# A hybrid decoder step on one core: five matmuls a k tile, and block products that add up in PSUM

## The reference

```
h = modulate(rms_norm(x));  x = x + 0.5 * gate1 * swiglu(h, gate, up, down)      # ffn1, hidden width 2816
h = modulate(rms_norm(x));  z = h @ w_in
x = x + gate2 * (merge(conv branch, linear attention branch) @ w_out)            # "out"
h = modulate(rms_norm(x));  x = x + 0.5 * gate3 * swiglu(h, gate, up, down)      # ffn2
y = modulate(rms_norm(x));  swiglu(h) = (silu(h @ w_gate) * (h @ w_up)) @ w_down
```

## Time and profile before

| | us |
|---|---|
| median of three runs | 1432.65 |
| the runs | 1431.9 to 1434.09 |
| span of the profiled execution (the page gives no other time for it) | 1432.1 |
| TensorE busy | 1389.1 (97%) |
| DVE busy | 977.2 (68%) |
| ACT busy | 539.3 (38%) |

### The profile page before, as it was taken

How to read it: one execution, slowest core, us unless ns; L and a number is a source line. 1 busy time by engine, 2 the same in 40 slices (tenths; PEclk the granted TensorE clock), 3 DMA queues, 4 the chain that set the end, 5 groups by cost and what they waited for, 6 DMA issues and landing times.

```text
span 1432.1 us, 28796 instructions
## 1 busy us (share of the span) xinstructions
PE 1389.1 (97%) x11782; PEld 1344.0 (94%) x11782; DVE 977.2 (68%) x1731; ACT 539.3 (38%) x797; POOL 80.2 (6%) x120
## 2 busy tenths in 40 slices
PE   6999999999999999999999999999999999999996
PEld 5899999999998999999899897999899999999996
DVE  6446675357547588998998997854554776456745
ACT  5423343224336222524243237422352344224433
POOL 6100000010001000000000000100000000000000
PEclk9999999999999999999999999999999999999998
DMA  9754646454364223213334453626312332323321
GB/s 322 237 177 155 205 149 206 147 168 142 103 208 142 89 88 93 89 60 104 125 128 146 136 169 127 220 91 198 104 59 74 92 117 89 114 76 106 101 77 60
DMA packets 132701, 189.49 MB, mean 132 GB/s; under 512 B 4621, under 2 KB 112545, under 8 KB 132386
## 3 DMA queue, kind: packets, MB, share of 16 engines
q1 hardware_dynamic: 111388, 112.54, 25.0%
q0 software_dynamic: 17136, 66.87, 14.0%
q10 hardware_dynamic: 4070, 8.57, 1.6%
HBM read 173.73 MB, written 15.18 MB: 132 GB/s over the span
## 4 chain that ended last, share of the span: by engine, by line
PE 84%; DVE 10%; ACT 3%; issue 2%; DMA 1%; POOL 0%; DVEq 0%; ACTq 0%
PE pu L646 51%; PE pu L828 13%; PE pu L817 11%; PE pu L660 2%; PE pg L690 2%; DVE w_lo L1680 1%; DMA work<-in_w_ada 1%; PE pg L1064 1%; ACT w_hi L1227 1%; DVE d L2106 1%; DVE w_lo L1969 1%; DVE work L2216 1%; PE pg L726 0%; DVE work L2215 0%; DVE work L2227 0%
## 5 line engine op out<-in xcount | busy, mean ns | idle before, releaser
L1680 DVE TENSOR_TENSOR w_lo<-raw,w_hi 128x1024 fp32r<-128x1024 f32 x152 | 186.1, 1225 | 255.5 <-ACT w_hi L1227 255.4
L1227 ACT CAST w_hi<-raw 128x1024 fp32r<-128x1024 f32 x152 | 158.9, 1046 | 412.0 <-PE pu L646 373.0
L646 PE MATMUL pu<-h_hi,w_hi 128*128 128x260 f32 x1408 | 288.4, 286 | 4.6 <-DVE work L2381 2.8
L646 PE MATMUL pu<-h_hi,w_lo 128*128 128x260 f32 x1408 | 284.1, 283 | 0.0
L646 PE MATMUL pu<-h_lo,w_hi 128*128 128x260 f32 x1408 | 283.3, 283 | 0.0
L646 PEld LDWEIGHTS pu<-h_hi,w_hi 128*128 128x128 f32 x1408 | 217.7, 189 | 8.7 <-DVE w_lo L1680 4.8
L646 PEld LDWEIGHTS pu<-h_hi,w_lo 128*128 128x128 f32 x1408 | 217.4, 189 | 0.0
L646 PEld LDWEIGHTS pu<-h_lo,w_hi 128*128 128x128 f32 x1408 | 217.2, 189 | 0.0
L2106 DVE SCALAR_TENSOR_TENSOR d<-u,cw,d 128x512 f32<-128x512 f32 x240 | 163.2, 745 | 0.1
L646 PE MATMUL pu<-f_hi,w_hi 128*128 128x260 f32 x704 | 142.9, 284 | 0.0
L646 PE MATMUL pu<-f_hi,w_lo 128*128 128x260 f32 x704 | 141.8, 283 | 0.0
(11 more groups left out here) (352 smaller groups left out, 2369.7 us busy)
## 6 DMA issues: line engine op xcount, KB each, us to landing
raw_a<-in_w_ada POOLq DMA_DIRECT2D x30, 1024.0 KB, 7.9
raw<-in_w_in SPq DMA_DIRECT2D x28, 1024.0 KB, 5.2
raw<-in_ffn_up SPq DMA_DIRECT2D x22, 1024.0 KB, 5.3
raw<-in_ffn_gate SPq DMA_DIRECT2D x21, 1024.0 KB, 5.3
raw<-in_ffn_down SPq DMA_DIRECT2D x16, 1024.0 KB, 5.1
gates_d<-sg ACTq DMA_DIRECT2D x24, 260.0 KB, 2.4
raw<-in_ffn_down SPq DMA_DIRECT2D x8, 768.0 KB, 4.4
work<-gates_d POOLq DMA_DIRECT2D x2, 2080.0 KB, 8.8
```

What stands on the lines that cost most here:

```text
L646: last = mm(pu[p][:, e, 0:HALF], w[p][:, k, :], m[:, k, e * HALF:(e + 1) * HALF], start=(k == 0 and j == 0), stop=(k == k_tiles - 1 and j ...
L1227: nc.scalar.copy(w_hi[p][:], raw[:, slot, :, p * P:(p + 1) * P]).then_inc(s_hi, 1)
L1680: V.tensor_tensor(w_lo[p][:], raw[:, slot, :, p * P:(p + 1) * P], w_hi[p][:].bitcast(F32), ALU.subtract).then_inc(s_lo, 1)
```

## The change

1. The down units and "out" are computed by `unit_uneven`: LEFT = 276 columns lie in one bank, the other REST = 244 twice in the other bank. w_hi meets h_hi's and h_lo's 244 columns in one matmul of 2 x 244 = 488 columns, whose two sums lie side by side; w_lo h_hi is added to the first of them. That makes five matmuls a k tile: 276, 488, 276, 276, 244. So that one operand can take in both, h_hi and h_lo become halves of one tensor, and f_hi and f_lo too.
2. `residual` adds both sums of 244: three scalar_tensor_tensors (236, 276 and 236 columns) and three small steps, with waits on a new semaphore between.
3. P1, P6, P7 and P4 are accumulated in one bank, and P5 and P3 in another. ACT copies the running sum out as p1, u2 and u3 and takes P4's by its Silu directly; DVE keeps three additions (c11 = p1 + P2, c22 = u3 + P5, c12 = u2 + (P5 + P3)). P2 lies in the other pair's first bank, and the pairs change roles from turn to turn. U0A comes before P4 and P3. ACT's Silu of the second tile is in two halves.
4. At the first turn of a group the wait for `s_evac[1]` stands ahead of P2.

Two semaphores of the spilled rows of x are made one, without another order. In the diff the up blocks' code (`up_half`, the halves of `up_unit`), DVE's three additions (in point 3) and renamed waits are left out.

```diff
+LEFT = 276
+REST = N - LEFT
...
-P1, P2, P6, P5, P7, P4, P3, U0A, U0B, U1A, U1B = range(TURN)
+P1, P2, P6, P5, P7, U0A, P4, P3, U0B, U1A, U1B = range(TURN)
+UP_BLOCKS = (U0A, U0B, U1A, U1B)
...
-        h_hi = sb("h_hi", [P, KT, N], F32R)
-        h_lo = sb("h_lo", [P, KT, N], F32R)
+        h2 = sb("h2", [P, 2, KT, N], F32R)
+        h_hi, h_lo = h2[:, 0], h2[:, 1]
...
+        f2, work = overlay(("f2", [P, 2, KT, N], F32R), ("work", [P, BF], F32))
...
+            def unit_uneven(n, p, both, k_tiles=KT, ready=None):
+
+                weights_and_psum(n, p)
+                hi, lo = both[:, 0], both[:, 1]
+                left, rest = pu[p][:, 0, 0:LEFT], pu[p][:, 1, 0:2 * REST]
+                for k in range(k_tiles):
+                    if ready is not None:
+                        s, v, first = ready
+                        if k == 0 and first > 1:
+                            pe.wait_ge(s, v + first)
+                        elif k >= first or k == 0:
+                            pe.wait_ge(s, v + k + 1)
+                    start, stop = k == 0, k == k_tiles - 1
+                    mm(left, w_hi[p][:, k, :], hi[:, k, 0:LEFT], start=start, stop=False)
+                    mm(rest.rearrange("p (s n) -> p s n", s=2), w_hi[p][:, k, :], both[:, :, k, LEFT:N],
+                       start=start, stop=False)
+                    mm(left, w_hi[p][:, k, :], lo[:, k, 0:LEFT], start=False, stop=False)
+                    mm(left, w_lo[p][:, k, :], hi[:, k, 0:LEFT], start=False, stop=stop)
+                    last = mm(rest[:, 0:REST], w_lo[p][:, k, :], hi[:, k, LEFT:N], start=False, stop=stop)
+                last.then_inc(s_done, 1)
...
-            def product(j, bank, hi, lo):
+            def product(j, bank, hi, lo, start=True):
 
                 pe.wait_ge(s_blo, j + 1)
                 for k in range(4):
                     for n, (w, m) in enumerate(((w_hi, hi), (w_hi, lo), (w_lo, hi))):
                         last = mm(bank, w_block(w, j)[:, k, :], m[:, k, :],
-                                  start=(k == 0 and n == 0), stop=(k == 3 and n == 2))
+                                  start=(start and k == 0 and n == 0), stop=(k == 3 and n == 2),
+                                  skip_group_check=not start)
                 last.then_inc(s_bd, 1)
...
-                    a0, a1, b0, b1 = (pu[p][:, e, 0:HALF] for p in range(2) for e in range(2))
+                    own, other = it % 2, 1 - it % 2
+                    a, b, c = pu[own][:, 0, 0:HALF], pu[other][:, 0, 0:HALF], pu[own][:, 1, 0:HALF]
                     m = ADA_UP[g] + 2 * it if which == 1 else LATE0
                     if it == 0:
                         pe.wait_ge(s_evac[0], at[f"down{which}_{g}"] // 2)
                     else:
                         pe.wait_ge(s_um, 2 * t - 1)
-                    product(j + P1, a0, h_block(h_hi, 0, 0), h_block(h_lo, 0, 0))
-                    product(j + P2, a1, h_block(h_hi, 1, 0), h_block(h_lo, 1, 0))
+                    product(j + P1, a, h_block(h_hi, 0, 0), h_block(h_lo, 0, 0))
                     if it == 0:
                         pe.wait_ge(s_evac[1], at[f"down{which}_{g}"] // 2)
                     else:
                         pe.wait_ge(s_um, 2 * t)
+                    product(j + P2, b, h_block(h_hi, 1, 0), h_block(h_lo, 1, 0))
                     pe.wait_ge(s_tl, 4 * which)
-                    product(j + P6, b0, t_hi[:, 1], t_lo[:, 1])
-                    product(j + P5, b1, t_hi[:, 0], t_lo[:, 0])
                     pe.wait_ge(s_p1, t + 1)
-                    product(j + P7, a0, t_hi[:, 2], t_lo[:, 2])
+                    product(j + P6, a, t_hi[:, 1], t_lo[:, 1], start=False)
+                    product(j + P5, c, t_hi[:, 0], t_lo[:, 0])
+                    pe.wait_ge(s_u2, t + 1)
+                    product(j + P7, a, t_hi[:, 2], t_lo[:, 2], start=False)
                     pe.wait_ge(s_c11, t + 1)
-                    product(j + P4, a1, t_hi[:, 3], t_lo[:, 3])
+                    up_half(j + U0A, other, 0)
                     if m < LATE0:
                         ada(Lin(m))
                         ada(Lin(m + 1))
-                    pe.wait_ge(s_u2, t + 1)
-                    product(j + P3, b0, h_block(h_hi, 1, 1), h_block(h_lo, 1, 1))
                     pe.wait_ge(s_u3, t + 1)
-                    pe.wait_ge(s_c2, t + 1)
-                    up_unit(j + U0A, 0)
+                    product(j + P4, a, t_hi[:, 3], t_lo[:, 3], start=False)
+                    pe.wait_ge(s_c22, t + 1)
+                    product(j + P3, c, h_block(h_hi, 1, 1), h_block(h_lo, 1, 1), start=False)
+                    up_half(j + U0B, other, 1)
                     if m < LATE0:
                         ada_transpose(Lin(m))
                         ada_transpose(Lin(m + 1))
-                    pe.wait_ge(s_v2, t + 1)
+                    pe.wait_ge(s_sg, 3 * t + 1)
                     pe.wait_ge(s_c12, t + 1)
-                    up_unit(j + U1A, 1)
+                    up_half(j + U1A, own, 0)
+                    up_half(j + U1B, own, 1)
...
-                            unit(Lin(at["down2_2"] + c), c % 2, f_hi, f_lo, GROUPS[g],
-                                 ready=(s_a, a0, GROUPS[g] - 1) if c == 0 else None)
+                            unit_uneven(Lin(at["down2_2"] + c), c % 2, f2, GROUPS[g],
+                                        ready=(s_a, a0, GROUPS[g] - 1) if c == 0 else None)
...
+                    a = pu[it % 2][:, 0, 0:HALF]
                     for pos in range(TURN):
                         act.wait_ge(s_bd, TURN * t + pos + 1)
                         if pos == P1:
-                            nc.scalar.copy(p1, pu[0][:, 0, 0:HALF]).then_inc(s_p1, 1)
+                            nc.scalar.copy(p1, a).then_inc(s_p1, 1)
+                        if pos == P6:
+                            nc.scalar.copy(u2, a).then_inc(s_u2, 1)
+                        if pos == P7:
+                            nc.scalar.copy(u3, a).then_inc(s_u3, 1)
+                        if pos == P4:
+                            af(sg[:, 1, 0:HALF], a, ACT.Silu).then_inc(s_sg, 1)
...
-            def residual(n, m, gt):
+            def residual(n, m, gt, r):
 
                 p = n.base % 2
                 g = lambda a, b: flat(mod[:, bass.ds(m + 8 * gt, 1), a:b])
-                ps = pu[p]
-                V.scalar_tensor_tensor(tile(x, m, 0, HALF), ps[:, 0, 0:HALF], g(0, 1), tile(x, m, 0, HALF),
-                                       ALU.mult, ALU.add)
-                V.scalar_tensor_tensor(tile(x, m, HALF, NP), ps[:, 1, 0:NP - HALF], g(0, 1), tile(x, m, HALF, NP),
-                                       ALU.mult, ALU.add)
-                V.tensor_tensor(t8[:, p, :], ps[:, 1, NP - HALF:HALF], g(1, 9), ALU.mult).then_inc(s_evac[p], 1)
-                dve.wait_ge(s_evac[p], n.half().value(1, 1))
-                V.tensor_tensor(tile(x, m, NP, N), tile(x, m, NP, N), t8[:, p, :], ALU.add).then_inc(s_x, 1)
+                left, hi, lo = pu[p][:, 0, 0:LEFT], pu[p][:, 1, 0:NP - LEFT], pu[p][:, 1, REST:REST + NP - LEFT]
+                samples = pu[p][:, 1, 0:2 * REST].rearrange("p (s n) -> p s n", s=2)[:, :, NP - LEFT:REST]
+                V.scalar_tensor_tensor(tile(x, m, LEFT, NP), hi, g(0, 1), tile(x, m, LEFT, NP), ALU.mult, ALU.add
+                                       ).then_inc(s_res, 1)
+                V.scalar_tensor_tensor(tile(x, m, 0, LEFT), left, g(0, 1), tile(x, m, 0, LEFT), ALU.mult, ALU.add)
+                V.tensor_tensor(t8[:, p], samples, g(1, 9).unsqueeze(1).to_broadcast([P, 2, NS]), ALU.mult
+                                ).then_inc(s_res, 1)
+                dve.wait_ge(s_res, r.value(3, 1))
+                V.scalar_tensor_tensor(tile(x, m, LEFT, NP), lo, g(0, 1), tile(x, m, LEFT, NP), ALU.mult, ALU.add
+                                       ).then_inc(s_evac[p], 1)
+                dve.wait_ge(s_res, r.value(3, 2))
+                V.tensor_tensor(t8[:, p, 0, :], t8[:, p, 0, :], t8[:, p, 1, :], ALU.add).then_inc(s_res, 1)
+                dve.wait_ge(s_res, r.value(3, 3))
+                V.tensor_tensor(tile(x, m, NP, N), tile(x, m, NP, N), t8[:, p, 0, :], ALU.add).then_inc(s_x, 1)
```

More of the change, by code:

```diff
@@ L184, in decoder_step @@
         assert off <= BF
[L185 to L190, removed]
+        f2, work = overlay(("f2", [P, 2, KT, N], F32R), ("work", [P, BF], F32))
+        f_hi, f_lo = f2[:, 0], f2[:, 1]
         def wk(name):
@@ L223, in decoder_step @@
         sg = sb("sg", [P, 4, N])
-        p1, u2, v2, u3 = (sg[:, 2 + j // 2, j % 2 * HALF:(j % 2 + 1) * HALF] for j in range(4))
+        p1, u2, u3 = (sg[:, 2 + j // 2, j % 2 * HALF:(j % 2 + 1) * HALF] for j in range(3))
         mod = sb("mod", [P, NADA, 10])
@@ L817, in product, with up_half @@
                         last = mm(bank, w_block(w, j)[:, k, :], m[:, k, :],
-                                  start=(k == 0 and n == 0), stop=(k == 3 and n == 2))
```

(40 more changed lines are left out.)

58 lines of the change are left out of this document (25 added, 33 removed).

## The result

| | before | after |
|---|---|---|
| median of 4 runs, us | 1433.06 (1431.90 to 1434.09) | 1449.55 (1447.80 to 1451.87) |
| profiled execution, us | span 1432.1 | 1448.31, span 1446.6 |

The ratio is 1.0114, with a 95% interval from 1.0101 to 1.0127: 16.5 us slower, where 4.4 were forecast, and 3.5 us beyond the top of the range. The two spans differ by 14.5 us, and that is what the trace can account for. One run of experiment 5's first kernel, 1938.31 us at a mean clock of 0.654, is left out of its numbers.

What follows compares the result with a forecast made beforehand. TensorE, busy for 97% of the span with matmuls 120 ns apart, was taken to bound the kernel. The sum -14.2 + 10.8 + 1.7 + 6.1 = +4.4 us on the median 1432.65 gave 1437.0 us, range 1427 to 1446.

Steps and rivals of the forecast that it cites:

- Part 1: K tiles of down and output units: with a 120 ns floor, five matmuls take 686 ns against 720, saving 14.2 us.
- D: Rival, k tiles: 488 columns in two runs cost two short matmuls, nothing saved; +17.8 us, 1450.5; chance 0.05.
- A: Rival, k tiles: a fee per matmul at full clock, saving only 4.9 us; +13.2 us, 1445.8; chance 0.20.
- Part 2: Products in PSUM: steady turns stay at 21.58 us, the added short waits being covered by slack.
- The up slab has more: Steady turns: the gate slab's arrival is hidden by 1.9 us, and the up slab has more slack than that.
- Part 3: First turns of groups 1 and 2: P2 waits for the longer evacuation, stalls 3.9 and 2.2 us; +10.8 us for four entries.
- Part 4: Ends of ffn1, the output units and ffn2: the longer residual is on the chain, 3 x 0.56 = +1.7 us.
- Part 5: Clock at the four entries: a half-clock stage behind each stall, 1.5 us each, +6.1 us; bounds 0 and 6.1.

Runs made afterwards that it cites:

- experiment 5's first kernel: The changed kernel with DVE's residual ahead of the two weight-block splits in the last two down units of groups 0 and 1: 1439.81 us, ratio 1.0035.
- experiment 5: Residual ahead of weight blocks: in the changed kernel 1439.81 us, new turns alone 1432.91, five-matmul units alone 1435.54, kernel before 1432.27.
- experiment 3: The changed kernel with the 488-column matmul taken apart into two of 244 columns, six matmuls a k tile: 1448.71 us, ratio 1.0116 to the kernel before.
- experiment 1: The changed kernel with streams of 20 fp32r matmuls, 64 to 488 columns, behind its end: 107 ns for 64, 119 for 260, 226 for 488.
- experiment 2: The changed kernel with streams of 20 fp32r matmuls of other widths, 192 to 512 columns, behind its end: 188 ns for 416, 202 for 448, 217 for 480.

## Why the prediction was wrong

The direction was right, the time was not, and one term makes the difference. By its parts:

- **Part 1, the step that failed.** "I read the 120 as a floor set by a weight load running beside a stream" gave 206 ns for 488 columns and 120 for 276, 34 ns a tile, 14.2 us. Measured: 3.4 ns a tile saved in the down units of 8 k tiles, 0.22 us for eight units and 0.9 for all 32, nothing in those of 6, some 0.1 in the output units: about 0.8 us in all. Taking the 488 apart again costs 1.3 ns a tile (experiment 3), and a smaller weight load saves nothing (experiment 1). Time goes by columns, about 0.45 ns each, and the columns are the same before and after. The two rows that spoke for the floor misled. At half clock 217 ns is slower than 260 x 0.45, so that limit is hidden. The matmuls of L1021 are of another operand type, and their price wasn't fp32r's; each has two records in the trace, and that one record stands for 520 columns was assumed, no run shows it. Both rows lay near the question by number and were far from it in kind. With 0.8 in place of 14.2 the forecast's own sum is +17.8 us, where 16.5 were measured.
- Of the rivals D ("nothing is saved", 1450.5, chance 0.05) is what happened to within 1 us, though not by its mechanism: two short matmuls cost 228, not 240, and the long one 220. That its total is so near is in part luck: its sum has four half-clock stages, and the trace has three. A (a fee, 1445.8) is refuted by 416, 448 and 480 columns, which are 5 to 7 ns above it. The Trainium skill (TensorE: Matmul & The Clock Gate, Back-to-back issue gap) prices an isolated full-clock matmul by its columns too, plus 2.5 ns; with that page's weight load (LDWEIGHTS) the prediction's estimate was 665 ns for a tile before and after. That the two hardly differ the trace bears out, with 720.8 and 717.4. The 2.4 columns a ns it doesn't: 512 fp32r columns are 228 to 233 ns, where the rule gives 215.8.
- **Part 2** held in the steady turns: 21.61 us against 21.58. But "The up slab has more" was too sure: in the second turn of group 2, ffn1, ACT waited 2.90 us for it, and through the copy of P6 that reached TensorE, 0.46 us before 340.24.
- **Part 3** held in place and nearly in size: stalls of 1.9 and 1.9 at group 2 (2.2 forecast), 3.2 and 0.33 + 2.34 at group 1 (3.9 forecast). The turns lost 14.1 us, 4.5 of it the clock's; the other 9.6 compare with 10.8. At group 1 of ffn2 P1 itself waited, for the evacuation of the unit before, which wasn't foreseen: it begins 0.5 us later than at the pace of the tiles. The units of 6 k tiles showed no wait of their own, but one output unit did, 0.3 us before 1013.86, for the longer residual. Experiment 5 shows the cause at the entries: the queue on DVE.
- **Part 4**: 1.3 for 1.7. At the end of ffn2 the chain from L1873 at 1431.82 to the first matmul of the last sums at 1434.22 is 2.40 us, against 1.96 before (1417.14 to 1419.10), 0.44 each.
- **Part 5**: three stages of 1.5, 4.5 us for 6.1. How many come is a matter of the execution: the same entries brought four in the trace of experiment 2 (one of them 6.83 us long) and two in that of experiment 3.

With the measured sizes, -0.8 + 9.6 + 1.3 + 4.5 = +14.6, of a span 14.5 longer. The two waits outside the turns add 0.8, and the stretches in front of group 1 and behind the last sums take 1.0 off, which none of the parts explains.

## What to carry to other kernels

Before a matmul is merged or resized, find out whether its time goes by columns or by a floor: only below the floor (here 107 to 114 ns, up to 244 columns) can merging pay. Rows of another operand type or at another clock don't answer that, and a stream of 20 does. Where a wait moves to an earlier consumer, look at what stands ahead of the producer in its engine's queue: here two instructions that weren't yet needed, with the wait for their input, made the whole loss of the new turns alone, and moving the producer ahead of them gave it back. Where the producer was made longer as well, 6.2 us stayed.

## What the hardware showed that was not expected

- From 260 columns on, fp32r matmuls with new weights each time are 0.445 to 0.463 ns a column apart with the clock granted in full, where 2.4 GHz is 0.417, and at half clock 217 ns for 260 columns, which is 1.2 GHz.
- A moving operand in two runs isn't slower than in one: 220 against 226 ns for 488 columns.
- Idle time alone doesn't tell whether the clock falls. 1.90 us before 311.07 brought no stage and 1.91 before 1295.92 one of 3.4 us; at the first of these places 1.90 us did bring one in experiment 2's trace (313.60). In the middle of every kernel here stands a wait of 1.97 to 2.01 us (1.98 before 924.15 in the kernel before), the same code each time: seven of the eleven traces have a stage behind it, four have none. What else decides was not tried.
- Nor does it take idle time. In experiment 1 the granted clock fell to 0.50 for 6.83 us in streams without a hole, behind 20 matmuls of 64 columns and some of 128, in the first and third series and not in the second.
- So runs of one kernel differ by whole stages. The changed kernel's four are in the order of their mean granted clock: 1447.80 us at 0.988, 1448.31 at 0.987, 1450.79 at 0.986, 1451.87 at 0.985. An estimate: 0.003 of 1448 us is what two or three stages of 3.4 us at half clock take off, and they cost 3 to 4.5 us.
